# One 8 MB weight transfer of a sixteen-expert layer cut into pieces of 128, 49, 64 and 15 rows

## The reference

```python
def ec_moe(h, router_w, w_gu, w_down):
    cap = EC_CAPACITY_FACTOR * n // N_EXPERTS                  # 2 * 256 // 16 = 32 tokens per expert
    logits = jnp.einsum('bnd,de->bne', h, router_w, ...)
    aff = jax.nn.softmax(logits, axis=-1)
    gates, idx = lax.top_k(jnp.swapaxes(aff, 1, 2), cap)       # each expert takes its best 32 tokens
    def expert(args):
        xe, wgu, wd = args                                     # wgu 1024 x 4096, wd 2048 x 1024
        gu = jnp.einsum('bcd,df->bcf', xe, wgu)
        ga, up = jnp.split(gu, 2, axis=-1)
        return jnp.einsum('bcf,fd->bcd', jax.nn.silu(ga) * up, wd)
    ...                                                        # each row times its gate, added to its token
```

## Time and profile before

| | us |
|---|---|
| median of three timed runs | 1488.76 |
| the profiled execution's own time | 1486.36 |
| its span (first to last instruction) | 1484.6 |
| TensorE busy | 1147.1 (77%) |
| VectorE busy | 468.4 (32%) |
| ScalarE busy | 398.3 (27%) |
| bytes moved, over the span | 503.33 MB, 339 GB/s |

### The profile page before, as it was taken

How to read it: one execution, slowest core, us unless ns; L and a number is a source line. 1 busy time by engine, 2 the same in 40 slices (tenths; PEclk the granted TensorE clock), 3 DMA queues, 4 the chain that set the end, 5 groups by cost and what they waited for, 6 DMA issues and landing times.

```text
span 1484.6 us, 19383 instructions
## 1 busy us (share of the span) xinstructions
PE 1147.1 (77%) x8336; PEld 754.3 (51%) x8336; DVE 468.4 (32%) x954; ACT 398.3 (27%) x890; POOL 74.1 (5%) x89
## 2 busy tenths in 40 slices
PE   9999999999999998995566466566665564565677
PEld 7888988888877875442322223223222232232234
DVE  6575777656788764110000000000000000000002
ACT  5665567555657642110000000000000000000002
POOL 0000020000035411000000000000000000000000
PEclk9999999999999998798778778787887787887789
DMA  8435546555553488999999999999999999999996
GB/s 313 171 138 203 198 172 223 208 207 199 199 187 114 149 347 343 397 436 434 433 437 426 433 433 435 424 442 430 430 437 426 438 430 433 433 426 440 423 424 288
DMA packets 29450, 503.33 MB, mean 339 GB/s; under 512 B 4275, under 2 KB 4915, under 8 KB 8245
## 3 DMA queue, kind: packets, MB, share of 16 engines
q1 hardware_dynamic: 25344, 493.43, 79.7%
q10 hardware_dynamic: 4020, 8.66, 1.6%
HBM read 501.03 MB, written 1.05 MB: 338 GB/s over the span
## 4 chain that ended last, share of the span: by engine, by line
issue 60%; PE 32%; DVE 5%; ACT 1%; POOL 1%; POOLq 0%; DVEq 0%; ACTq 0%
PE PB L378 9%; PE PB L358 5%; PE PB L359 5%; PE PB L360 5%; PE PB L379 4%; DVE SPL L1575 1%; DVE XN L1595 0%; PE PB L409 0%; POOL SP L2238 0%; PE PB L815 0%; PE PB L680 0%; PE PB L418 0%; PE PB L507 0%; PE PB L799 0%; PE PB L454 0%
## 5 line engine op out<-in xcount | busy, mean ns | idle before, releaser
L919 PE MATMUL PB<-RING,XS 128*32 128x512 f32 x2048 | 292.8, 720 | 177.0 <-DMA RING<-in_wgu_dram 176.7
L919 PEld LDWEIGHTS PB<-RING,XS 128*32 128x32 f32 x2048 | 68.4, 126 | 345.3 <-issue 249.8
L951 PE MATMUL PB<-RING,HHT 128*32 128x256 f32 x2048 | 150.9, 452 | 111.9 <-DMA RING<-in_wdn_dram 110.5
L1575 DVE TENSOR_TENSOR SPL<-RAW,SPH 128x512 fp32r<-128x512 f32 x318 | 207.0, 709 | 31.4 <-ACT SPH L1048 28.7
L378 PE MATMUL PB<-XT,SPH 128*128 128x512 f32 x544 | 194.1, 401 | 0.0
L1048 ACT ACTIVATE SPH<-RAW 128x512 fp32r<-128x512 f32 x340 | 186.8, 620 | 7.4 <-DMA RAW<-in_wst_dram 3.3
L951 PEld LDWEIGHTS PB<-RING,HHT 128*32 128x32 f32 x2048 | 75.3, 129 | 172.2 <-issue 141.7
L379 PE MATMUL PB<-XT,SPL 128*128 128x256 f32 x544 | 152.4, 280 | 0.0
L1506 ACT ACTIVATE SG<-PB 128x512 f32<-128x512 f32 x16 | 9.6, 597 | 506.1 <-PE PB L919 506.1
L2128 DVE SCALAR_TENSOR_TENSOR YL<-PB,COLS,YH 128x256 fp32r<-128x256 f32 x64 | 31.0, 484 | 279.0 <-ACT YH L1520 279.0
L378 PEld LDWEIGHTS PB<-XT,SPH 128*128 128x128 f32 x544 | 102.2, 188 | 24.6
(11 more groups left out here) (398 smaller groups left out, 1577.5 us busy)
## 6 DMA issues: line engine op xcount, KB each, us to landing
RAW<-in_wst_dram SPq DMA_DIRECT2D x84, 1024.0 KB, 4.9
RING<-in_wgu_dram SPq DMA_DIRECT2D x13, 2048.0 KB, 40.4
RING<-in_wgu_dram SPq DMA_DIRECT2D x4, 4096.0 KB, 22.3
RING<-in_wgu_dram SPq DMA_DIRECT2D x14, 1024.0 KB, 8.1
RING<-in_wdn_dram SPq DMA_DIRECT2D x6, 2048.0 KB, 13.4
RING<-in_wdn_dram SPq DMA_DIRECT2D x2, 4096.0 KB, 19.0
RING<-in_wdn_dram SPq DMA_DIRECT2D x3, 1024.0 KB, 41.0
RAW<-in_wst_dram SPq DMA_DIRECT2D x4, 256.0 KB, 5.6
```

The lines of the kernel that those rows point to most:

```text
L919: i = e.matmul(PB[b][32 * c:32 * c + 32, :], XS[x % 2][:, k, :], chunk_at(n)[:, 512 * c:512 * c + 512], start=k == 0, stop=k == KD - 1)
L951: w = e.matmul(PB[b][32 * j:32 * j + 32, 0:T], HHT[:, j, 32 * c:32 * c + 32], chunk_at(n)[:, T * (4 * (c % 2) + j):T * (4 * (c % 2) + j + ...
L1575: e.tensor_tensor(l, src, h.bitcast(F32), ALU.subtract).then_inc(*lo.up())
```

## The change

The change touches one of the 8 MB transfers: the first one of expert 14 (`x = 14`, `j = 0`, slot 2). In place of one transfer of 128 rows of 64 KB there are four. The first brings the first 36 KB of all 128 rows. The other three bring the last 28 KB of each row: rows 0 to 48 (49 rows, on seven DMA engines), rows 49 to 112 (64 rows) and rows 113 to 127 (15 rows). They are issued one behind the other, with no wait between them. Each adds 16 to `s_ring[0]`, so the number that TensorE waits for before the first eight chunks of expert 14 grows by 48.

```diff
         if e < 15:
-            return s_ring[g // 2], 16 * (e - 1 - (g < 2))
+            return s_ring[g // 2], 16 * (e - 1 - (g < 2)) + (48 if e == 14 and g < 2 else 0)
...
+        def uneven(x, j):
+
+            ring, pair = PAIR[SLOT_OF[2 * j] // 2], io["wgu"][2 * x + j]
+            cut = 36 * 256
+            e.dma_start(ring[:, 0:cut], pair[:, 0:cut]).then_inc(s_ring[j], 16)
+            for a, b in ((0, 49), (49, 113), (113, 128)):
+                e.dma_start(ring[a:b, cut:8 * UNIT], pair[a:b, cut:8 * UNIT]).then_inc(s_ring[j], 16)
+
         for x in range(3, 15):
             for j in range(3):
                 e.wait_ge(*moe.at(("chunk", x - 1, 8 * j + 7)))
-                whole(x, j)
+                if (x, j) == (14, 0):
+                    uneven(x, j)
+                else:
+                    whole(x, j)
```

## The result

The changed kernel takes 1511.66 us, the median of four runs (1510.96 to 1516.74), against 1488.77 for the kernel before. The ratio is 1.0174, with a 95% interval from 1.0159 to 1.0189: slower by 1.7%. The two medians are 22.9 us apart, the spans of the two profiled executions 24.5 us (1509.1 against 1484.6), and the ratio makes about 26 us; the expectations further down say 23. The forecast was 1486.5, a gain of 2.2 us, and its range ended at 1491.5. It was wrong in its sign, and ten times too small in size.

A forecast was written before the change was run, and what follows sets the result against it. Weight transfers were taken as the bound, with eight late DMA engines setting the end. The last landing moves 2.2 us earlier, sharing, semaphore and hidden issues add 0: 1488.76 - 2.2 = 1486.5 us, 8-in-10 range 1481.6 to 1491.5.

The forecast's parts named there:

- What bounds the kernel: From expert 1 on, full-rate weight transfers bound the kernel; eight late DMA engines set its end, half idle the last 6 to 8 us.
- Who moves how much: Cut transfer: seven engines get 12 rows (+4.24 us), eight get 5 (-3.18 us), one gets 4 (-4.24 us), instead of eight each.
- Which engines are the seven: In the cut transfer, the seven engines given extra rows were assumed to be seven of the eight that finish early.
- rival C: All or some of the seven engines with extra rows are late ones, ending at 1479.2: 1493.0 us, chance 0.08.
- A place in SBUF written by two engines: In the cut pieces, engines writing neighbouring SBUF rows together cost nothing: 0 us taken, bounds 0 and +7.4 us.
- Rival A: Late part is SBUF, not an engine, so helpers can't shorten the late landings: 1488.8 us, chance 0.22.
- Rival B: In the 49-row piece, engines sharing a place slow down and the seven end last: up to +7.4 us, 1493.9, chance 0.12.
- Rival D: Landings move as planned but TensorE's work before the end can't start earlier: gain below 1 us, 1488, chance 0.08.
- The semaphore and SyncE's issues: At the cut transfer, TensorE's wait for four transfers costs 0 us; SyncE's three extra issues take 1.0 us, hidden.
- Where the gap comes from: Queue 8's 28 instruction packets, about 1.2 us each, may delay eight engines by 4 us by 1332 us; not shown.

The follow-up runs named there:

- e2_halves: Against the kernel before: expert 14's 28 KB tails go as rows 0 to 63 and rows 64 to 127, each on sixteen engines; 1501.21 us, ratio 1.0095.

## Why the prediction was wrong

*What bounds the kernel* was right. The stream runs full, half of the engines end 6 us early, and TensorE waits for the late ones.

*Who moves how much* was right: 12, 5 and 4 rows. The 54 completions count the engines of each piece, and the transfer behind the copies into HBM ends in the groups that follow from it.

*Which engines are the seven* failed. They were taken as seven of the eight early ones. The runs show five early and two late. The two set the end: +4.24 us for their four rows more, where the sum had -2.2. This was rival C in its weaker form ("or some of them are"). It had a chance of 0.08, and its price fits: the same shapes in HBM cost 13.5 us where 8.5 would be an even share, and the copy on seven engines moved the end by about what it added. The Trainium skill (DMA: Bandwidth & Descriptors, "The descriptor swizzle") has engines 0 to 7 on rows 0 to 63 of a full transfer; no run here shows an engine's number. The prediction put that beside its eight early engines and read "low numbers" as "early". No row stood behind that.

*A place in SBUF written by two engines* failed, and it is the large term. The prediction took 0 between the bounds 0 and +7.4. The upper bound was not one: it halved the rate of seven engines for seven rows, and counted nobody else. In the run the other engine of each pair is slowed as well, the pieces of 64 and 15 rows share too, and the following whole transfer is drawn in. On average an engine moved 14.0 GB/s for 45 us, against 27.0. The change costs 22.9 us by the medians and 25.9 by the ratio. If 4.2 of them are the two late engines, some 19 to 22 us remain for the sharing, where the sum had 0; the halves, with no uneven load at all, cost 14. The price is a difference and was not measured by itself in the changed kernel.

The Trainium skill (SBUF — State Buffer, "Door 1: The DMA port swizzle") has sixteen ports of eight partitions, 27.2 GB/s each, and rows 0 to 63 reach only eight. By it two halves of 64 rows run at half rate, and the trace agrees: 211 GB/s against 444. The prediction had read this rule rightly and drawn its conclusion: other engines can't bring the late rows sooner, "the sum would be 0 or a loss". It gave rivals A and B, which say so, 0.22 and 0.12, and took the gain at 0.50, because nothing in the trace told the two readings apart. The halves tell them apart: `e2_halves` run first would have shown it.

*Rival A* (the gap can't be bought back) was right in that a helper brings nothing to a full place, and wrong in its price, since it left out what the attempt costs. *Rival B* named the mechanism, with 7.4 us in place of some 20. *Rival D* played no part: the landing before expert 14 and the span's end moved by nearly the same time, 24.8 and 24.5 us.

*The semaphore and SyncE's issues* held: three issues in 1.65 us in place of 1.0, hidden.

*Where the gap comes from* was left open, with queue 8 as a reading. The trace of the kernel before shows it. These are the late eight's completions of the transfer before the cut one (1355.7 to 1356.3 us); then the packets from 1362 to 1369 us, with one of queue 8; then, of the transfer after the cut one, the late completions from 1394.4 to 1395.5 and from 1396 to 1396.4 us:

```profile
DMA packets 18, 0.66 MB, mean 1092 GB/s; under 512 B 8, under 2 KB 8, under 8 KB 8
...
q8 instruction: 1, 0.02, 0.9%
...
DMA packets 14, 0.52 MB, mean 477 GB/s; under 512 B 6, under 2 KB 6, under 8 KB 6
...
DMA packets 5, 0.20 MB, mean 492 GB/s; under 512 B 2, under 2 KB 2, under 8 KB 2
```

Eight stand together. Behind the instruction packet of 1363 us they are 7 and 1, the one about 1.5 us later, and behind the next one, at 1385 us, 6 and 2. So it goes all the way: from 711 to 1369 us there are 28 instruction packets, each puts back one of the sixteen completions by about 1.5 us, and from 770 us on it is always one of the same eight, in turn. That makes 28 x 1.5 / 8 = 5.3 us for each, nearly the whole gap; the prediction's estimate was 4. Each of the early eight shifts by 1 us at most against the others in that time. So the lag is a loss of the engine, as the prediction argued against rival A. It still can't be bought back late in the stream, for by that reading of the halves a place in SBUF takes no more from two engines than from one (26.4 GB/s).

## What to carry to other kernels

In this kernel a transfer into SBUF ran at full rate only when each engine wrote the rows that it writes in all the others. Cutting 128 rows into pieces of fewer rows made engines share, and that halved the rate, for the neighbours in the queue too; cutting along the row was free (0.9998). Who wants to hand work from a slow helper to a fast one should first see which part is slow, and try the helping alone. When a bound for an unknown price is made, count everyone who shares the resource, and everything that is queued behind them. And a busy share of 1.0 says nothing about the rate (here it stood beside 198 GB/s): read the bytes beside it.

## What the runs showed of the hardware

Sixteen engines on 64 rows moved 211 GB/s, and on 128 rows 444. A copy from HBM to HBM of 7 whole rows of 64 KB used all sixteen engines, in packets of 28 KB; with rows of 63 KB at a distance of 64 KB it used seven, and two of them ended last. Stopping the stream once costs 2.9 us (1489.55 against 1486.61), with an interval that reaches from 0 to 5. It evens out the engines for the rest of the run, but it doesn't pay. Each 16 KB instruction packet put one of eight engines back by about 1.5 us; why these eight, and which numbers they have, stays open, and no run moved those packets. How the 19 to 22 us of sharing divide between the pieces and the transfer behind them is known only by the run with the stopped stream (15.4 us for the pieces, the two late engines' part included). No version here beats the kernel before.
